# Prompt attention of a two-layer decoder step: the compressed branch's four query tiles of two heads as one unit

## The reference, cut to what matters

```
sc = einsum('btghd,bjgd->bghtj', q, kc) * scale - slope * dist_c     # compressed: 31 blocks
pc = masked_softmax(sc, dist_c >= 0)      # exp(s - max), / max(sum, 1e-30)
oc = einsum('bghtj,bjgd->btghd', pc, vc)
... the same for the selected branch (osel) and the window branch (ow)
out = g0 * oc + g1 * osel + g2 * ow       # g: sigmoid of the gates
```

## Time and profile before

| | |
|---|---|
| median of three executions | 2332.9 us |
| profiled execution, its own time | 2321.67 us, span 2319.9 us, mean granted clock of TensorE 0.985 |
| PE busy over the whole span | 2228.1 us (96%) |
| DVE / ACT / GpSimd busy over the whole span | 1244.8 / 664.7 / 262.4 us |
| prompt attention (first scores to last values) | 195.9 to 396.6 us |
| PE / DVE / ACT busy from 253 to 277 us, 24 us | 21.81 / 20.74 / 19.42 us |

### The profile page before, as it was taken

One profiled execution on the slowest core, in us unless ns is written; L12 is line 12 of the kernel. 1 busy time (PEld: TensorE's weight loads), 2 busy tenths in 40 slices (PEclk: granted clock), 3 DMA queues, 4 the chain that ended last, 5 costly groups with the idle time before them and its releaser, 6 DMA issues.

```text
span 2319.9 us, 31053 instructions
## 1 busy us (share of the span) xinstructions
PE 2228.1 (96%) x11218; PEld 1710.0 (74%) x11218; DVE 1244.8 (54%) x3249; ACT 664.7 (29%) x1652; POOL 262.4 (11%) x498
## 2 busy tenths in 40 slices
PE   8998998888898999999999999999999999999998
PEld 7655555666576888888888775667778888888887
DVE  1016887555347777777723341243477677777323
ACT  2005886444222222222100220244232222220002
POOL 1002000000001222222000000130022222220000
PEclk9999999999899999999999999999999999999999
DMA  8126201696421232222222213222223222322223
GB/s 201 49 79 208 69 2 38 173 229 175 85 77 37 83 100 73 73 88 95 73 73 91 77 42 91 56 63 75 78 75 103 79 73 74 108 74 73 77 87 106
DMA packets 205818, 207.62 MB, mean 89 GB/s; under 512 B 40394, under 2 KB 192178, under 8 KB 205410
## 3 DMA queue, kind: packets, MB, share of 16 engines
q1 hardware_dynamic: 201650, 187.87, 28.2%
q0 software_dynamic: 4016, 17.75, 2.3%
HBM read 194.23 MB, written 19.69 MB: 92 GB/s over the span
## 4 chain that ended last, share of the span: by engine, by line
PE 90%; DVE 5%; issue 3%; ACT 2%; DMA 0%; DVEq 0%; SPq 0%; ACTq 0%
PE PS L2405 53%; PE PS L2287 4%; PE PS L1305 3%; PE PS L2374 3%; PE PS L2258 3%; PE PS L1391 2%; PE PS L1344 2%; PE PS L1530 2%; PE PS L589 2%; PE PS L603 2%; PE PS L663 2%; PE PS L2227 1%; PE PS L621 1%; PE PS L651 1%; PE PS L677 1%
## 5 line engine op out<-in xcount | busy, mean ns | idle before, releaser
L2405 PE MATMUL PS<-HT,ring 128*128 128x272 f32 x1536 | 373.7, 393 | 0.0
L2405 PE MATMUL PS<-arena,ring 128*128 128x272 f32 x1392 | 341.8, 392 | 0.0
L2405 PEld LDWEIGHTS PS<-HT,ring 128*128 128x128 f32 x1536 | 292.7, 191 | 60.7
L2405 PEld LDWEIGHTS PS<-arena,ring 128*128 128x128 f32 x1392 | 264.3, 190 | 54.5
L2713 ACT ACTIVATE arena<-arena,CB,CW 128x560 f32<-128x560 f32 x128 | 109.3, 854 | 382.6 <-DVE arena L3039 315.9
L2405 PE MATMUL PS<-arena 128*128 128x272 f32 x768 | 195.6, 398 | 12.7 <-DVE arena L2981 12.7
L2405 PE MATMUL PS<-arena,CONST 128*128 128x272 f32 x768 | 191.7, 392 | 0.0
L3054 DVE SCALAR_TENSOR_TENSOR arena<-arena,CW 128x560 f32<-128x560 f32 x256 | 187.3, 789 | 0.0
L2405 PEld LDWEIGHTS PS<-arena 128*128 128x128 f32 x768 | 147.9, 193 | 44.1 <-issue 13.3
L2405 PEld LDWEIGHTS PS<-arena,CONST 128*128 128x128 f32 x768 | 145.9, 190 | 30.1
L3220 POOL COPY arena<-arena 128x16 f32<-128x16 f32 x128 | 50.9, 397 | 637.6 <-DVE arena L3039 536.7
(11 more groups left out here) (451 smaller groups left out, 3476.8 us busy)
## 6 DMA issues: line engine op xcount, KB each, us to landing
ring<-in_w_ffn_up SPq DMA_DIRECT2D x64, 1024.0 KB, 6.4
ring<-in_w_ffn_down SPq DMA_DIRECT2D x32, 1024.0 KB, 5.0
ring<-in_cache_nsa_kv SPq DMA_DIRECT2D x128, 128.0 KB, 3.7
arena<-in_cache_nsa_kv SPq DMA_DIRECT2D x56, 256.0 KB, 6.9
ring<-in_w_ml_in SPq DMA_DIRECT2D x12, 1024.0 KB, 5.4
arena<-in_cache_nsa_win SPq DMA_DIRECT2D x16, 512.0 KB, 5.7
out_nsa_win_sample<-in_cache_nsa_win POOLq DMA_DIRECT2D x8, 1016.0 KB, 19.3
ring<-in_w_nsa_in SPq DMA_DIRECT2D x6, 1024.0 KB, 5.7
```

Source lines behind the costliest of these rows:

```text
L2405: last = mm(PS[:, bank, 0:HALF], lhs[:, k, :], rhs(k), start=(first and k == 0), stop=(done and k == 3))
```

## The change

The compressed branch of a head pair becomes one unit for all four query tiles, placed first: 9 units for a head pair and 72 in all. The scores of tile c stand in columns 32c to 32c+30 of one 128-wide piece for each head. DVE adds the distances, takes the maximum of each tile and head, subtracts it, and after the exponential sums, clamps, inverts, multiplies by the gate and weighs, each in one instruction for two heads and four tiles, each linked to the next. The 128 columns are turned at once. As the turned piece then holds the rows of all four tiles, the values get four copies (VCZ), each zero outside the 31 rows of its tile; the product for tile 0 is made in the unit's own `values`, those of tiles 2, 3 and 1 in the `values` of that tile's selected branch. VCZ lies in the part of KVP that has been stored to HBM: GpSimd sets it to zero between the first and the second store.

```
+        UNITS = [(0, 0)] + [(i, br) for i in (0, 2, 3, 1) for br in (1, 2)]
+        PAIRS = [(n, i, br) for n in range(8) for i, br in UNITS]
...
# PE, scores
+                if br == 0:
+                    for c in range(4):
+                        for g2 in range(2):
+                            rows = slice(64 * g2, 64 * g2 + 64)
+                            last = mm(PS[:, 2 * (p % 2) + g2, 32 * c:32 * c + NCMP_P], QT[rows, n, c * P:(c + 1) * P],
+                                      KCT[rows, n // 4, 0:NCMP_P], start=True, stop=True)
+                            if c == 3:
+                                last.then_inc(s_qk, 1)
+                    return
...
# PE, turn_probs
-                    if br == 0:
-                        last = tr(PS[0:NCMP_P, 4 + g2, 0:P], PB[:, u % 6, 0:NCMP_P], ident)
-                    else:
-                        for k in range(i + 1):
...
+                    for k in range(1 if br == 0 else i + 1):
...
# PE, values
+                def compressed(g2):
+                    out = PS[64 * g2:64 * g2 + 64, 6 + n % 2, i * P:(i + 1) * P]
+                    c0 = gp * P + 64 * g2
+                    return mm(out, VCZ[:, i, c0:c0 + 64], PTC[n % 2][:, g2, :], start=True, stop=False)
+
+                if br == 0 or (br == 1 and i):
                     for g2 in range(2):
...
+                        last = compressed(g2)
...
# ACT
+                            copy(PTC[n % 2][:, g2, :], PS[:, 4 + g2, 0:P]).then_inc(s_te, 1)
...
+                        nc.scalar.activation(by_block(PB[:, 2 * (p % 3):2 * (p % 3) + 2, 0:P]),
+                                             by_block(SB[:, 2 * (p % 2):2 * (p % 2) + 2, 0:P]), ACT.Exp).then_inc(s_ex, 2)
...
# DVE, blocks
-                v.tensor_copy(VC[0:NCMP, :], PS[0:NCMP, 3, 128:384]).then_inc(s_kce, 1)
+                dve.wait_ge(s_cjz, 2)
+                for c in range(4):
+                    last = v.tensor_copy(VCZ[32 * c:32 * c + NCMP_P, c, :], PS[0:NCMP_P, 3, 128:384])
+                last.then_inc(s_kce, 1)
...
# DVE, biased
+                    fc.link(v.tensor_tensor(sb, by_block(PS[:, 2 * (p % 2):2 * (p % 2) + 2, 0:P]), BC[:, n % 2], ALU.add))
+                    fc.link(v.tensor_reduce(peak, sb, AX, ALU.max))
+                    fc.link(v.tensor_scalar(peak, peak, FLOOR, None, ALU.max))
+                    v.tensor_tensor(sb, sb, peak.unsqueeze(3).to_broadcast([P, 2, 4, NCMP_P]), ALU.subtract)\
+                        .then_inc(s_tt, 2)
...
# DVE, weighed
-                    fc.link(v.tensor_scalar(st[:, 1, :], st[:, 1, :], 1e-30, None, ALU.max))
+                    fc.link(v.tensor_reduce(total, pb, AX, ALU.add))
+                    fc.link(v.tensor_scalar(total, total, 1e-30, None, ALU.max))
+                    fc.link(v.reciprocal(total, total))
+                    fc.link(v.tensor_tensor(total, total, G[:, 0:4, c:c + 13:12].rearrange("p i g -> p g i"), ALU.mult))
+                    v.tensor_tensor(pb, pb, total.unsqueeze(3).to_broadcast([P, 2, 4, NCMP_P]), ALU.mult)\
+                        .then_inc(s_sc, 2)
...
+            v.memset(PB[:, :, 31:P:32], 0.0)
...
-                if p % 12 == 6 and p // 12 < 7:
+                if p % NU == 5 and p // NU < 7:
...
-                if p % 12 == 4 and p > 12 and p < NP:
+                if p % NU == 3 and p > NU and p < NP:
...
# GpSimd
                 if c:
                     pool.wait_ge(s_kvp, 16)
+                    g.memset(VCZ, 0.0).then_inc(s_cjz, 1)
```

More of the change, by code:

```diff
@@ L271, in trunk @@
         ST = a(4 * 6, "p (s f g) -> p s f g", s=4, f=3)
+        VCZ = KVP[:, :, 0:256]
+        PTC = [KVP[:, s, 256:512].rearrange("p (g c) -> p g c", g=2) for s in range(2)]
+        BST = [KVP[:, 2 + s, 256:272].rearrange("p (f g i) -> p f g i", f=2, g=2) for s in range(2)]
         b_ = area(ct_at)
@@ L429, in trunk @@
         s_fp, s_fo = sem("s_fp"), sem("s_fo")
-        PAIRS = [(n, i, br) for n in range(8) for i in (0, 2, 3, 1) for br in range(3)]
+        UNITS = [(0, 0)] + [(i, br) for i in (0, 2, 3, 1) for br in (1, 2)]
+        PAIRS = [(n, i, br) for n in range(8) for i, br in UNITS]
+        NU = len(UNITS)
         NP = len(PAIRS)
@@ L472, in unit_width, with by_block @@
         def unit_width(br, i):
-            return NCMP_P if br == 0 else (i + 1) * P
+            return P if br == 0 else (i + 1) * P
+        def by_block(ap):
+            return ap.rearrange("p g (i j) -> p g i j", j=32)[:, :, :, 0:NCMP_P]
         def turned(a_, bank):
@@ L585, in scores @@
                     pe.wait_ge(s_tt, 2 * (p - 1))
+                if br == 0:
[7 more added lines that the diff above has]
+                    return
                 for g2 in range(2):
                     rows = slice(64 * g2, 64 * g2 + 64)
-                    key = KCT[rows, n // 4, 0:w] if br == 0 else KTS[rows, br - 1, n // 4, 0:w]
-                    mm(PS[:, 2 * (p % 2) + g2, 0:w], QT[rows, n, i * P:(i + 1) * P], key, start=True, stop=True)\
-                        .then_inc(s_qk, 1)
+                    mm(PS[:, 2 * (p % 2) + g2, 0:w], QT[rows, n, i * P:(i + 1) * P], KTS[rows, br - 1, n // 4, 0:w],
+                       start=True, stop=True).then_inc(s_qk, 1)
             def turn_probs(p):
@@ L608, in values @@
                 gp = n // 4
-                if p % 12 == 0 and n >= 2:
+                if p % NU == 0 and n >= 2:
                     pe.wait_ge(s_ot, n - 1)
                 pe.wait_ge(s_te, 2 * p + 2)
-                for k in range(1 if br == 0 else i + 1):
-                    for g2 in range(2):
[L614 to L619, removed]
+                def compressed(g2):
[3 more added lines that the diff above has]
+                if br == 0 or (br == 1 and i):
+                    for g2 in range(2):
+                        last = compressed(g2)
+                if br:
+                    for k in range(i + 1):
+                        for g2 in range(2):
+                            out = PS[64 * g2:64 * g2 + 64, 6 + n % 2, i * P:(i + 1) * P]
                             c0 = 256 + 512 * br + gp * P + 64 * g2
-                            last = mm(out, KVP[:, k, c0:c0 + 64], PTS[:, u % 4, k * P:(k + 1) * P],
+                            last = mm(out, KVP[:, k, c0:c0 + 64], PTS[:, (2 * p + g2) % 4, k * P:(k + 1) * P],
                                       start=False, stop=(br == 2 and k == i))
```

30 lines of the change are left out of this document (23 added, 7 removed).

## The result

The changed kernel takes 2306.9 us, the median of 4 runs (2305.66 to 2311.53), against 2333.5 for the kernel before, the median of 4 (2329.15 to 2334.72): ratio 0.990, 95% interval 0.988 to 0.992. The two profiled executions are closer together: 2321.67 before and 2305.66 after, 16.0 us.

What follows compares the result with a forecast made beforehand. PE and DVE were taken to bound the prompt's attention in turns. Eight head pairs 1.47 us shorter gave -11.8, plus 1.2, 0.4 and 0.5 added: -9.7 us, from 2332.9 to 2323, range 2312 to 2331.

Steps and rivals of the forecast that it cites:

- (a): Start of a head pair: PE's eight products for compressed scores and the way to DVE, 1.6 us.
- (b): DVE's chain next: new `biased`, last unit's `weighed`, a 128-wide `biased`, new `weighed`, then to PE: 4.43 us.
- (c): PE next: turn 0.37, last unit's values 0.6, tile 2's scores 0.84, then 0.2 us to DVE.
- (d): DVE runs on to the start of `weighed` of tile 3's first unit: 9.0 us, from 10.59 before.
- (e): From that `weighed` of tile 3's first unit on DVE to PE's turn: 0.79 us.
- (f): PE's turns, values and scores to the end of the head pair: 4.72 us, making 22.5 in all.
- The unknown rows of DVE: New wide DVE steps without a measured row: full-width steps 0.42 us, reductions of 248 elements 0.41.
- The start: Ahead of and in the first head pair: three more value copies 1.2 us, longer pieces at low clock 0.4.
- The end: After the last scores, values of sixteen products remain instead of a short one: 0.5 us added.
- Rival 1: PE runs ahead, DVE's and PE's new waits don't appear: period 21.2 us, kernel 2313; chance 0.10.
- The step that failed: Applying the forecast difference to the median of the other executions: 2332.9 - 9.7 = 2323 us.
- rival 2: More low clock in the prompt's attention: another 5.1 us falls on the changed kernel, 2328; chance 0.15.

Runs made afterwards that it cites:

- double_reduce: Changed kernel with the new unit's maximum reduction in `biased` done twice on DVE: head pair 22.59 us instead of 22.13, median moved by only 0.7.
- start_table: Changed kernel with first scores waiting for the keys' copy alone and ACT's exponential table loaded early: 2305.9 us.
- after_again: The changed kernel, unchanged, run again: 2309.5 us, mean clock 0.985 to 0.987.
- held_first: Changed kernel with three added clears on DVE ahead of the new unit's `weighed`, lengthening PE's wait among short rows: 2318.9 us.
- before_out_later: Kernel before the change with its copy of finished output moved six units later, shortening PE's longest wait: 2322.7 us.
- tables_gap: Changed kernel with the bias tables made three units later, in DVE's idle time: one execution 2299.4 us, three 2306.4 to 2307.2.
- held: Changed kernel with two added clears on DVE behind the bias tables, lengthening PE's wait before tile 3's turns: 2313.6 us.
- held_mid: Changed kernel with two added clears on DVE at the third unit, ahead of tile 2's wide turns: 2313.3 us.
- before_again: Kernel before the change, unchanged, twelve executions: nine at 2332.4 to 2334.8 us (the usual kind), three at 2323.0 to 2326.2.

## Why the prediction was wrong

Step by step:

- What bounds the stretch: right. PE and DVE wait for each other, and double_reduce shows that an added 0.41 us on DVE makes a head pair 0.46 longer.
- (a) to PE's scores and DVE's start, 1.6 us: mis-sized. It is 1.26 (246.03 to 247.29). I took 0.34 for each of four rows of four products, but that includes the change to another row; sixteen in one row take 1.02 from start to start, where 1.36 stood. This is 0.34 x 8 = 2.7 us too little gain, and nearly all of the period's error (22.1 against 22.5).
- (b) 4.43 forecast, 4.42 measured (247.29 to 251.71). (c) 1.99 (to 253.70), as forecast. (d) 8.92 for 9.0. (e) 0.80 for 0.79. (f) 4.75 for 4.72. The unknown rows of DVE are 0.41 to 0.42, the value taken. The Trainium skill, "VectorE: DVE Perf Modes", section "The perf-mode tier table (the rule you actually need)", has reductions at one element a cycle; the 411 and 405 ns for 248 elements, as much as the 417 of the two-input step, agree.
- The start: copies 1.3 for 1.2. The first head pair is 25.87 us (198.04 to 223.91) where 24.6 stood in the profiled execution before, 1.3 more and not 0.4. The table load that ran ahead is now in its path, and DVE waits 1.37 for it. I listed ACT's work as lying beside the rest and didn't follow its first instruction. start_table takes it away together with the copies, and 2.8 us go. How much of the 1.3 is the load's is not settled, since much of this head pair runs at the low clock and its length goes with that: it is 27.7 us in the usual execution before and 24.9 in after_again.
- The end: 0.5 more was forecast behind the last scores. From the last head pair's first scores to the end of the stretch it is some 0.6 less beside the period's 1.8 (25.5 us, against 31.1 before, 3.1 of them low clock).
- Rival 1 is the one whose number (2313) came nearest, but not what happened: DVE's wait at (a) is 1.64 us, PE's at (c) 0.27, and the period is 22.1, not 21.2.
- **The step that failed** is the last one: "That execution was 11 us below the median of the three others, so I apply the difference to the median." That holds only if what made the profiled execution faster stays the same in both kernels. Most of it was low clock in this very stretch: 211.5 us in a usual execution, 203.2 in the profiled one. I had even read 5.1 us of it and took it as something that could only be added (rival 2), never taken away; the sum has no term for it. Yet in the changed kernel the 1.15 us wait behind which the clock fell is 0.41, and the clock is 1.00 in every steady head pair.

In numbers, first between the two profiled executions: 15.9 us. Of these, 5.1 are what the one before had beyond its 23.97 us period. Not all of that is low clock, as the prediction has it: between 324.67 and 348.99 the clock is full and PE waits 0.30 for DVE once more, which costs 0.4. The other 10.8 are the chain: 12.8 for seven shorter periods and 0.6 at the end, less 1.3 of copies and 1.3 of the first head pair. The forecast's 9.7 stands against these 10.8.

Between the usual execution before and after_again it is 24.7: 9.8 that the seven head pairs behind the first had beyond their period (9.4 of low clock, and the same 0.4), 13.4 for the period and the end, less 1.3 up to the first scores, and 2.8 less in the first head pair, where both run at the low clock for most of the time (18.2 and 13.5 us of it). So the mechanism of the chain was right and close in size; the 9.4 us of low clock, and part of the 2.8, are what the last step left out.

That low clock of this size follows from PE's waits is shown for the changed kernel by held_first. That the shorter wait is what took the drops out of the kernel before is argued from held_first and before_out_later together, and not shown: the drops could not be taken away from it without also shortening its chain, and in before_out_later some stayed.

Still open: why a wait of 1.65 us among long rows leaves the clock alone, why the same waits bring it down in one head pair and not in the next, whether the place of the waits counts or their rhythm, and why three of four executions of tables_gap have a lower clock.

## What to carry to other kernels

Before a difference is applied to a median, ask why the profiled execution is not at the median: compare the mean granted clock of all runs, and if one stretch has a low clock in some of them, count it among what the change can remove or add. A chain followed wait by wait gave the period within 2%, where each row had a neighbour; the error was in the price of a row's beginning, so take a row's length from start to start in a row of the same length. Where the first unit of a loop changes, follow each engine's first instruction, its table load too.

## What the runs showed of the hardware

- In the steady head pairs of these kernels the clock fell to 1.2 GHz only behind two waits of PE close together among short rows: 0.32 then 1.15 us (five of seven head pairs in the usual execution before, two of seven in the profiled one), 0.31 then 0.56 (one of seven, before_out_later), 0.31 then 1.44 (five of seven, held_first). It lasted about 3.5 us, in the last head pair of the kernel before about 7, and 3.5 us of it cost 0.8 to 1.5 us. Waits of 1.65 and 1.20 us among longer rows (held, held_mid) brought none, nor did 0.31 then 0.27 in the changed kernel. In the same kernel it varies between executions: 2323.0 us at a mean clock of 0.986 and 2334.7 at 0.979 in before_again.
- ACT's table load takes 1.28 us. In the changed kernel it stands behind the wait of the activation that needs it (201.83, 7.53 us of idle time before it); in the kernel before it ran ahead of that wait (193.46), and so it does in start_table (193.14).
- Reductions of 248 float32 elements to 8 take 405 to 411 ns on DVE, about the same as an add of that width (417), reading 31 of every 32 columns; the subtraction and the product that spread one value over 31 take 416 to 417 ns.
- Four copies of 31 rows to four different groups of partitions take 412 ns each, as one of 63 rows did (0.40).
